# One merged token-mixing block in place of three, with the last two input tiles and 12 conv taps moved into it

## The reference, cut to what matters

```python
h = rmsnorm(x, norms[0]) * (1 + sc1) + sh1
aq, ak, av, af, bq, bk, bv, bg, ca, cb = split_cols(jnp.dot(h, w_in))
logf = jax.nn.log_sigmoid((af + b_f).astype(F32))
o_a = attn_fn(aq, k_a, v_a, logf)                    # 4 heads x 128, causal softmax with a cumulative forget bias
q_b = rope(bq, pos); k_b = rope(bk, pos) * (DKB ** -0.5)
r, ret_s = retention(q_b, k_b, bv, ret_s0, ret_chunk) # 4 heads x 64, chunks of 128 rows, recurrent state
r = (_standardize(r).reshape(n, L, WB) * ret_gn_g.astype(F32)).astype(x.dtype)
o_b = r * jax.nn.silu(bg)
u = ca * jax.nn.sigmoid(cb)
cv, conv_state = causal_dwconv(conv_ctx, u, conv_w, conv_b)   # depthwise, 31 taps, 256 channels
o_c = jax.nn.silu(layernorm(cv, conv_ln_g, conv_ln_b))
mix = jnp.dot(jnp.concatenate([o_a, o_b, o_c], axis=-1), w_o)
```

## Time and profile before

| | us |
|---|---|
| median of 3 runs | 3267.7 (3264.27 to 3270.58) |
| the profiled execution | 3262.0 |
| its span in the trace | 3260.2 |
| project, layer 0 and layer 1 | 191.7 and 189.2 |
| retention, layer 0 | 76.0 |
| group norms, layer 0 | 42.2 |
| heads, layer 0 | 274.5 |
| samples, layer 0 | 54.6 |

### The profile page before, as it was taken

One profiled execution on the slowest core, in us unless ns is written; L12 is line 12 of the kernel. 1 busy time (PEld: TensorE's weight loads), 2 busy tenths in 40 slices (PEclk: granted clock), 3 DMA queues, 4 the chain that ended last, 5 costly groups with the idle time before them and its releaser, 6 DMA issues. The chain is left out here.

```text
span 3260.2 us, 45129 instructions
## 1 busy us (share of the span) xinstructions
PE 2951.3 (91%) x17756; PEld 2467.0 (76%) x17756; DVE 1751.8 (54%) x2765; ACT 1146.1 (35%) x1825; POOL 336.8 (10%) x166
## 2 busy tenths in 40 slices
PE   6798789979999999999767997998799999999996
PEld 3586477748878889999726865777388788899996
DVE  1396322243676676676615943223446766766765
ACT  1231123224444354444312311233235444454442
POOL 4111001013200000000042200100231000000000
PEclk7897699989999999999868966999799999999998
DMA  8311011143223332333182100111422333332331
GB/s 329 100 39 24 14 40 32 32 130 97 79 90 97 91 97 90 93 91 91 42 324 55 36 13 21 33 33 45 147 87 84 93 95 91 97 92 85 98 91 68
DMA packets 366283, 276.03 MB, mean 85 GB/s; under 512 B 24125, under 2 KB 308325, under 8 KB 365822
## 3 DMA queue, kind: packets, MB, share of 16 engines
q1 hardware_dynamic: 354896, 267.27, 26.3%
q10 hardware_dynamic: 11214, 6.41, 0.6%
HBM read 259.22 MB, written 15.26 MB: 84 GB/s over the span
## 5 line engine op out<-in xcount | busy, mean ns | idle before, releaser
L1536 PE MATMUL tslot<-g_hi,w_hi 128*128 128x260 f32 (+1 forms) x2496 | 672.9, 324 | 7.6 <-DVE g_lo L2065 6.1
L1536 PE MATMUL tslot<-g_hi,w_lo 128*128 128x260 f32 (+1 forms) x2496 | 667.0, 322 | 0.0
L1536 PE MATMUL tslot<-g_lo,w_hi 128*128 128x260 f32 (+1 forms) x2496 | 664.8, 321 | 0.0
L1536 PEld LDWEIGHTS tslot<-g_hi,w_hi 128*128 128x128 f32 x2496 | 416.4, 190 | 48.9 <-DVE g_lo L2065 6.2
L1536 PEld LDWEIGHTS tslot<-g_hi,w_lo 128*128 128x128 f32 x2496 | 415.4, 189 | 37.9
L1536 PEld LDWEIGHTS tslot<-g_lo,w_hi 128*128 128x128 f32 x2496 | 415.5, 190 | 37.4
L1507 ACT ACTIVATE w_hi<-w_raw 128x1024 fp32r<-128x1024 f32 x292 | 307.1, 1052 | 315.4 <-PE tslot L1854 311.8
L2126 DVE TENSOR_TENSOR cat<-cat,tslot 128x512 f32<-128x512 f32 (+1 forms) x320 | 220.4, 690 | 192.5 <-PE tslot L1854 191.3
L1511 DVE TENSOR_TENSOR w_lo<-w_raw,w_hi 128x1024 fp32r<-128x1024 f32 x256 | 311.8, 1218 | 0.0
L1854 PE MATMUL tslot<-f_hi,w_hi 128*128 128x260 f32 (+1 forms) x1056 | 283.6, 323 | 6.7 <-DVE w_lo L1511 4.5
L1854 PE MATMUL tslot<-f_hi,w_lo 128*128 128x260 f32 (+1 forms) x1056 | 282.0, 322 | 0.0
(11 more groups left out here) (320 smaller groups left out, 4052.8 us busy)
## 6 DMA issues: line engine op xcount, KB each, us to landing
w_raw<-in_ffn_up_dram SPq DMA_DIRECT2D x176, 512.0 KB, 3.7
a_raw<-in_ada_w_dram SPq DMA_DIRECT2D x24, 2048.0 KB, 17.1
w_raw<-in_ffn_down_dram SPq DMA_DIRECT2D x88, 512.0 KB, 3.3
w_raw<-in_w_in_dram SPq DMA_DIRECT2D x46, 512.0 KB, 3.9
w_raw<-in_w_o_dram SPq DMA_DIRECT2D x32, 512.0 KB, 3.7
kp<-in_cache_k_dram SPq DMA_DIRECT2D x32, 256.0 KB, 3.0
xrow<-in_x_prompt_dram SPq DMA_DIRECT2D x8, 512.0 KB, 8.8
out_k_prompt_dram<-k_tok SPq DMA_DIRECT2D x8, 512.0 KB
```

Source lines behind the costliest of these rows:

```text
L1536: last = pe.matmul(out[:, at + a:at + b], w[:, kk, :], x[:, kk, t0 + a:t0 + b], start=(kk == 0 and first), stop=(kk == KD - 1 and w is w_lo))
```

## The change

Project keeps 11 tiles: the forget gate, four conv tiles, q, q, k, k, v, v. The two gate tiles are made elsewhere. It keeps 50 of the 62 taps. The conv input now stands in rows 4 and 5 of the concatenated output `cat`, without zero columns: tap w reads fewer columns and adds them to a shifted part of the sum (`conv_tap`), so its width goes from 1024 down to 994. SP also writes the residual `x` (128 partitions of 8 x 1032 floats, 4.2 MB) to a DRAM tensor `x_hold`, and the samples block reads it back behind its own loads; in between the new block uses that memory for q, k, v, the bias and the turned probabilities.

`block_mixer` replaces retention, group norms and heads. It makes 14 tiles (12 of the heads, and the two gates last). Each tile is three *passes* over 344 columns with 24 matmuls each (L854). The passes are numbered p = 0 to 41, and behind each pass PE does a piece of the other work, by a fixed table; p = 42 to 45 have no pass. ACT, DVE, POOL and SP follow the same numbering. Retention stands at p = 0 to 9, the 12 taps at 1 to 12, the norms at 11 to 33, head h at 9 + 9h to 17 + 9h. The norms of the conv rows are summed by two matmuls each (one per row) where DVE added the rows first.

```diff
+TAPS_EARLY = 50
+def conv_tap(k, dve, n):
+    j, w = divmod(n, CONV_W)
+    w = CTX - w
+    u, acc = k.cat[:, 4 + j, :], k.cat[:, 6 + j, CTX - w:TP]
+    if w == CTX:
+        return dve.tensor_scalar(acc, u[:, 0:TP], k.vecs[:, 1, 2 * w + j:2 * w + j + 1], k.vecs[:, 0, V_CB + j:V_CB + j + 1],
+                                 ALU.mult, ALU.add)
+    return dve.scalar_tensor_tensor(acc, u[:, 0:TP - CTX + w], k.vecs[:, 1, 2 * w + j:2 * w + j + 1], acc, ALU.mult, ALU.add)
 def block_project(k, L):
-    tiles = [COL_CA, COL_CA + DC, COL_CA + P, COL_CA + DC + P] + [COL_BQ + P * j for j in range(8)]
+    tiles = [COL_CA, COL_CA + DC, COL_CA + P, COL_CA + DC + P] + [COL_BQ + P * j for j in range(6)]
-        u = sb("u", [P, 2, CTX + NT])
+        u = k.cat[:, 4:6, :]
-            for m, col in enumerate([COL_F] + tiles):
+            for m, col in enumerate([COL_F] + tiles + [2 * HA * DA]):
             sp.dma_start(d["conv_sample"][L, :, 0:CTX - 1, :], d["state_conv"][L, :, 1:CTX, :]).then_inc(stored, 16)
+            sp.dma_start(k.x_hold.rearrange("p (a b) -> p a b", b=NT), k.x[:, :, :]).then_inc(stored, 16)
-            sp.wait_ge(stored, 96)
+            sp.wait_ge(stored, 112)
-                taps(at, at + 8)
-                at += 8
+                if i < 7:
+                    taps(at, at + 8)
+                    at += 8
-            taps(at, len(todo))
+            assert at == TAPS_EARLY
+PASS = ((0, 344), (344, 688), (688, NT))
+N_TILES = 3 * HA + 2
+N_PASS = 3 * N_TILES
+def block_mixer(k, L):
+        LAST = N_PASS + 4
+        def phase(p):
+            h, at = divmod(p - 9, 9)
+            return (h, at) if p >= 9 and h < HA else (HA, p - 9 - 9 * HA) if p >= 9 else (-1, at)
+            # SP
+            def load(n):
+                if n >= 3:
+                    sp.wait_ge(lo_done, n - 2)
+                sp.dma_start(k.w_raw[n % 2][:, :, :], w_in[:, :, column(n):column(n) + P]).then_inc(loaded[n % 2], 16)
+            # PE
+            def dense_pass(p):
+                n, (a, b) = p // 3, PASS[p % 3]
+                if p % 3 == 0 and n >= 1:
+                    pe.wait_ge(lo_done, n)
+                if p >= 2:
+                    pe.wait_ge(evac, p - 1)
+                for kk in range(KD):
+                    for w, x, first in ((w_hi, k.h_hi, True), (w_hi, k.h_lo, False), (w_lo, k.h_hi, False)):
+                        last = pe.matmul(dense[p % 2][:, 0:b - a], w[:, kk, :], x[:, kk, a:b], start=(kk == 0 and first),
+                                         stop=(kk == KD - 1 and w is w_lo))
+                last.then_inc(pass_done, 1)
+            def attention(h, at):
+                if at == 0:
+                    if h >= 1:
+                        values(h - 1, 7)
+                    if h < HA:
+                        spread_bias(h)
+                        turn_values(h)
+                elif h == HA:
+                    return
+                elif at == 1:
+                    scores(h, 0)
+                    scores(h, 1)
+                    turn_keys(h)
+                elif at == 2:
+                    turn_probs(h, 0)
+                    turn_probs(h, 1)
+                    scores(h, 2)
+                    scores(h, 3)
...
+                elif at == 5:
+                    turn_probs(h, 4)
+                    scores(h, 6)
+                elif at == 6:
+                    values(h, 4)
+                    turn_probs(h, 5)
+                    scores(h, 7)
+                else:
+                    values(h, at - 2)
+                    turn_probs(h, at - 1)
+            for p in range(LAST):
+                if p < N_PASS:
+                    dense_pass(p)
+                h, at = phase(p)
+                if p == 0:
+                    samples()
+                if 2 <= p <= 9:
+                    back(p - 2)
+                if 1 <= p <= 8:
+                    front(p - 1)
+                if p >= 9:
+                    attention(h, at)
+                if 12 <= p < 21:
+                    norm_sums(p - 12)
+                if 11 <= p < 20:
+                    norm_mean(p - 11)
+                if 23 <= p < 32:
+                    norm_rows(p - 23)
+            # DVE, the start of its loop
+                if 1 <= p <= 8:
+                    prepare(p - 1)
+                if 1 <= p <= 2 * CONV_W - TAPS_EARLY:
+                    clink(conv_tap(k, dve, TAPS_EARLY + p - 1))
+                if 2 <= p <= 9:
+                    update(p - 2)
 def block_samples(k, L):
             ahead.load(sp)
+            sp.dma_start(k.x[:, :, :], k.x_hold.rearrange("p (a b) -> p a b", b=NT)).then_inc(x_back, 16)
+            sp.wait_ge(x_back, 16)
```

More of the change, by code:

```diff
@@ new lines, in turn_keys @@
+            def turn_keys(h):
+                pe.wait_ge(tok_moved, 3 * h + 1)
+                pe.wait_ge(evac, 9 * h + 9)
+                turn_blocks(kf[h % 2])
+                if h == 0:
+                    pe.wait_ge(r_moved, NC8)
+                else:
+                    pe.wait_ge(o_moved, NC8 * h)
+                for n, src in enumerate((kf[h % 2], vf)):
+                    last = pe.matmul(o_bank[0:S, P * n:P * n + P], src[:, TP:NT], ident, start=True, stop=True)
+                last.then_inc(turned, 1)
@@ new lines, in turn_probs @@
+            def turn_probs(h, i):
+                pe.wait_ge(normed, NC8 * h + i + 1)
+                if i < 2:
+                    pe.wait_ge(tok_moved, 3 * h + 2)
+                else:
+                    pe.wait_ge(p_moved, NC8 * h + (i - 1 if i < 4 else i))
+                for c in range(i + 1):
+                    to = score_cols(i)[0] + P * c
+                    last = pe.transpose(turn[:, to:to + P], prob[i % 2][:, P * c:P * c + P], ident)
+                last.then_inc(p_turned, 1)
@@ new lines, in _ @@
+            high(1)
+            for p in range(LAST):
+                h, at = phase(p)
+                if p < N_PASS:
+                    if p >= 9 and at == 0 and h < HA and h >= 1:
+                        attention(h, at)
+                    move_pass(p)
+                    if p % 3 == 2 and p // 3 + 2 < N_TILES:
+                        high(p // 3 + 2)
+                if 1 <= p <= 8:
+                    ret_values(p - 1)
+                if 2 <= p <= 9:
+                    ret_out(p - 2)
+                if p >= 9 and not (p < N_PASS and at == 0 and h < HA and h >= 1):
+                    attention(h, at)
+                if 11 <= p < 20:
+                    squares(p - 11)
+                if p == 33:
+                    for j in range(2):
+                        act.wait_ge(g_scaled, 11 + j)
+                        act.activation(k.cat[:, 6 + j, :], k.cat[:, 6 + j, :], ACT.Silu, scale=k.vecs[:, 0, V_LG + j:V_LG + j + 1],
+                                       bias=k.vecs[:, 0, V_LB + j:V_LB + j + 1]).then_inc(k.quiet, 1)
```

885 lines of the change are left out of this document (435 added, 450 removed).

## The result

The changed kernel takes 3096.17 us (median of 4 runs, 3091.52 to 3098.39). The kernel before took 3265.98 us on the same chip. The ratio is 0.9477, with a 95% interval of 0.946 to 0.9495. The gain is 169.8 us where 133 were forecast. The time lies 2 us under the low end of the range. The profiled execution has 3097.88 us.

The account below looks back on a forecast made before the run. PE was taken as the bound (busy 91%), at half clock in retention. Per layer 2.7 + 329.6 work + 17.5 waits = 349.8 us against 417.9, gain 68; two layers less 3 for x: 133, so 3135 us, range 3098 to 3205.

Parts of the forecast that it names:

- 1 and 4 (the clock falls): Clock falls in retention phases: 3189 us in part (0.17), 3261 in full (0.06); half clock well past retention: 3412 (0.04).
- 2 (the waits stay): Chains between engines outlast the passes, so PE idles 26.1 us per layer in place of 5: 3177 us, chance 0.09.
- 3 (x in the way): Transfers of x at 150 GB/s: write just fits, read ends 7 us after the present end; 3147 us, chance 0.05.
- 5 (project not shortened): Gate tiles and taps leave project without shortening it, as another engine ends at 290 too: 3177 us, chance 0.02.
- (a) to (e): Merged block's waits: half-clock starts 5 us, retention's chain covered, softmax chain 5, table loads 3, last phases 3; taken as 17.5.
- attention: PE work of the heads' attention in the merged block: 110 us per layer, same instructions after as before.
- norms: PE work of the norms in the merged block: 19.3 us by the clock, 24 with the added means and column sums.
- retention and samples' part: PE work in the merged block: 68.7 us at clock 0.52 becomes 37 if the clock holds at 1.00; lower end 34.
- tiles: Dense work in the merged block: 14 tiles x 11.33 = 158.6 us per layer at full clock.
- The softmax chain: Attention's maximum, exponential and normalizing, near 4.5 us for the widest block, mostly under passes; 5 us allowed for the rest.
- The table loads: Head 3: ACT alternates between Silu and exponential, 9 more loads per layer of 1.28 us; 3 us counted on the path.
- The half-clock start: PE starts at half clock twice, at the first pass and behind the samples' 32 tiny matmuls: 5 us.

## Why the prediction was right and where it was off

**The direction and the mechanisms held.** The clock was 1.00 in the retention phases with passes between, and the experiment with retention alone shows that without the passes it is 0.50. A phase of retention takes 8.5 us (forecast: about 8). "Without the pass each of the 8 chunks would wait 2.7" was measured as 2.68 ahead of six of the eight, in the experiment that took the pass away (a tap stands beside each chunk there; the kernel before, without taps, waited 7.3 us in all). The twelve taps were "worth nothing by themselves while PE is last", and 33 us with the gate tiles gone; the forecast had DVE end at 285 without their leaving, and in the run with 62 taps it ended at 279.5. Project took 152.5 us from its first product, 153.4 by the forecast.

**The rivals.** *1 and 4 (the clock falls)* did not happen: 1.00 from 276.8 to 597.7. *2 (the waits stay)* did not: 4.0 us. The run with attention in one piece shows their price where they do stay, 25 us of idle time per layer. *3 (x in the way)* did not, by the run without its transfers. *5 (project not shortened)* did not; it did come about once the taps were left in.

**The step that failed is the sum for the merged block:** allowances for waits most of which the passes cover, and the PE time of attention and norms carried over as if it were fixed. The sum was forecast at 329.6 + 17.5 = 347.1 us and took 329.5. By its terms:

| term of the sum, us | forecast | measured |
|---|---|---|
| (a) to (e), what PE still waits for | 17.5 | 4.0 |
| attention | 110 | 99.6 |
| norms | 24 | 17.8 |
| retention and samples' part | 37 | 40.4 |
| tiles | 158.6 | 167.7 |

*The waits* were mis-sized most. Of the five only (e), the last phases (3 us), is there, with 4.0. The softmax chain (5 us) costs nothing: no wait of PE ahead of the last phases. The table loads (3 us) happen and nobody waits for them; from ACT's timeline of the kernel after, in the last head:

```profile
577.04 1.28 ACT L1111 ACT_TABLE_LOAD   x1
...
579.19 1.28 ACT L1138 ACT_TABLE_LOAD   x1
```

The half-clock start (5 us) is no wait in the trace but longer matmuls; it comes once, from 274.0 to 276.8, costs 1.2 us inside "tiles" as measured, and there is no second one behind the samples' small matmuls. I had put small allowances on chains that I had just shown to be covered.

*Attention* was taken over as "the same instructions after as before". They are the same, but their PE time is not a constant: 109.5 us before, 99.6 in the changed kernel, and more in the run with attention in one piece, whose block needs 16.1 us more PE work. Busy time measured among waits contains the matmuls next to a wait. In the heads of the kernel before there are 66 in attention, and they take 7.8 us more than the others of their line and shape: a value product takes 0.21 us from start to start behind a wait, the others 0.11. In the changed kernel there are 6, with 0.7 us. That is 7.1 of the 9.9 us, and it could have been read from the trace before. The clock is 0.4 of it.

*Norms* were scaled by the clock, 26.1 x 0.74 = 19.3 us, and PE's time at 0.50 alone gives nearly the same, 19.7. But the doubled sums were put too high: the trace of the kernel before has 54 records of small column sums and that of the kernel after 72, so 18 more, which take 1.8 us (72 in 7.1), where the forecast worked from 36 and 3.8; and one more mean took 1.0 and not 1.9. The rest, some 4 us, is shorter PE time of the same steps in a stretch that had 16 us of idle time; what makes it shorter is not separated here.

*Retention* and *tiles* went the other way, +3.4 and +9.1. Retention was scaled by 0.52, but two matmuls of `back` that take 0.62 us at 0.50 take 0.36 at 1.00, 0.58 of it: busy time does not shrink in full with the clock. A pass takes 3.99 us (167.7 / 42) and not 3.78. Its first matmul is most of the difference. Two passes:

```profile
401.91 0.61 PE L854 MATMUL dense<-h_hi,w_hi 128*128 128x344 f32 x1
402.37 0.32 PE L854 MATMUL dense<-h_lo,w_hi 128*128 128x344 f32 x1
...
288.64 0.42 PE L854 MATMUL dense<-h_hi,w_hi 128*128 128x344 f32 x1
288.90 0.32 PE L854 MATMUL dense<-h_lo,w_hi 128*128 128x344 f32 x1
```

It takes 0.46 us to the next start behind matmuls of 384 columns and 0.26 behind ones of 128, 0.33 on the mean of the passes at full clock; the others take 0.157. 42 x 0.17 are 7.3 of the 9.1 us, the half clock at the start is 1.2. The forecast let every switch between kinds of work be free.

Together -13.5 - 10.4 - 6.2 + 3.4 + 9.1 = -17.6 us per layer, 35 in all, of the 37 by which the gain was larger. The last 2 are x: 1.5 us per layer were put on it, and the samples block grew by 0.5.

**Why the range was too narrow below.** Its low end let the waits go to 5 us and retention to 34, which gives 25 and 6 us. Attention and norms had no lower bound at all, because their PE time was read as work. With the floor that the kernel's own clock and waits suggest (some 10 and 6 us per layer, of which only the 7.8 us next to waits could be read beforehand) the low end would have been near 3070.

## What to carry to other kernels

Work that runs at half clock, or that waits for another engine in each step, gains twice from standing between pieces of dense work, and the two gains can be measured apart. When idle time is mixed away, take the busy time measured among the waits as an upper bound, not as a constant: here it fell by 9% in attention, most of it at the matmuls next to a wait, which a trace shows beforehand; and let each switch into a dense group cost 0.1 to 0.3 us. An edit that by the rows is worth nothing alone (twelve taps beside PE) can be worth 33 us behind another one, so cost each engine's end again after each part.

## What the runs showed of the hardware

- PE's busy share does not tell what keeps its clock. In the retention of the kernel before a stretch was busy 10.00 of 10.00 us at 0.50. With a pass of 24 matmuls over 344 columns between chunks of the same work, the clock stays at 1.00 through all the phases of retention, and 320.9 us in all (276.8 to 597.7). Which property of the small matmuls (64 rows or columns, 128 columns long) makes the difference was not tried, and no run starts the chunks alone at full clock without a wait.
- Short waits in attention can let the clock fall, and need not. In the run with attention in one piece the stretches behind waits of 1.5, 0.2, 1.5 and 0.5 us show 0.55 and 0.76 in the third head, and 1.00 behind the same waits in the second. The kernel before showed 1.00 in a stretch of 5 us that was busy 3.08.
- DVE's taps take 1.25 us each in the mixer, from DVE's groups in the mixer of the kernel after, and 1.52 in the kernel before, with up to 3% fewer columns. In project of the changed kernel eight of them take 12.48 us in one place, where POOL is busy for 3.33 us beside them, and 14.36 in the other, where it is busy for 6.54. No run here separates POOL's work from other causes. The group in the mixer:

```profile
L505 DVE SCALAR_TENSOR_TENSOR cat<-cat,vecs 128x1005 f32<-128x1005 f32 (+11 forms) x12 | 15.0, 1253 | 0.0
```

- The write of 4.2 MB left SP at 242.21 and the DMA engines were busy until about 257, some 15 us; the forecast took 20.
